# Layer 0 attention of a two-layer trunk: where projection units, modulation products and the turns at a head's end stand in TensorE's order

## The reference, cut to what matters

```python
mod = (silu(c) @ ada_w[l] + ada_b[l])[:, None, :]
h = rmsnorm(x, norm_g[l, 0]) * (1 + sc1) + sh1
proj = h @ w_in                       # even_mixer
# A: two score maps per head
s = where(causal, s - slope * dist, -inf); p = softmax(s)
w = p[:, :, 0] - lam * p[:, :, 1]
ya = rmsnorm(einsum(w, v), subln_g) * (1.0 - lam_init)
# B: dilated attention over three branches, heads in pairs
y = concatenate([ya, yb], axis=-1) @ w_out
```

## Time and profile before

| | us |
|---|---|
| median of 3 runs | 2991.62 (2991.14 to 2992.17) |
| profiled execution | 2992.33 |
| its span, first to last instruction | 2990.6 |
| mean granted clock of TensorE | 0.947 |
| layer 0's attention in the trace | about 106 to 663 |

### The profile page before, as it was taken

How to read it: one execution, slowest core, us unless ns; L and a number is a source line. 1 busy time by engine, 2 the same in 40 slices (tenths; PEclk the granted TensorE clock), 3 DMA queues, 4 the chain that set the end, 5 groups by cost and what they waited for, 6 DMA issues and landing times.

```text
span 2990.6 us, 35461 instructions
## 1 busy us (share of the span) xinstructions
PE 2687.0 (90%) x12576; PEld 2193.1 (73%) x12576; DVE 1261.9 (42%) x1451; ACT 1071.0 (36%) x1610; POOL 967.4 (32%) x402
## 2 busy tenths in 40 slices
PE   4999999989899999999999997666889999999995
PEld 2777778767678887788877786554667888788884
DVE  5566644333720155201567413766473005430145
ACT  2444443343433333333332223544343333322222
POOL 0111110004344444344434443211334444344442
PEclk7999999999899999999999998888999999999998
DMA  6233332043223332232346543111222333233232
GB/s 235 64 99 105 107 92 78 29 167 101 71 84 98 97 93 91 84 98 92 98 134 225 185 160 106 43 56 42 71 71 87 96 98 98 84 98 97 92 99 91
DMA packets 91097, 300.38 MB, mean 100 GB/s; under 512 B 9793, under 2 KB 10113, under 8 KB 91009
## 3 DMA queue, kind: packets, MB, share of 16 engines
q1 hardware_dynamic: 91008, 299.20, 31.4%
HBM read 275.05 MB, written 24.12 MB: 100 GB/s over the span
## 4 chain that ended last, share of the span: by engine, by line
issue 57%; PE 27%; POOL 11%; DVE 2%; DVEq 1%; ACT 1%; POOLq 1%; ACTq 0%
POOL w_lo L462 10%; PE ps L503 6%; PE ps L504 6%; PE ps L507 6%; PE ps L774 3%; PE ps L780 3%; PE ps L777 3%; POOL ybuf L473 1%; POOL arena L473 1%; DVEq L1222 0%; POOLq L476 0%; DVEq L1494 0%; DVE h_lo L1194 0%; ACT w_hi L828 0%; DVE ybuf L1186 0%
## 5 line engine op out<-in xcount | busy, mean ns | idle before, releaser
L462 POOL TENSOR_TENSOR w_lo<-w_raw,w_hi 128x1024 fp32r<-128x1024 f32 x370 | 909.4, 2461 | 1797.6 <-ACT w_hi L828 1293.5
L503 PE MATMUL ps<-h_hi,w_hi 128*128 128x512 f32 x2448 | 991.0, 405 | 85.8 <-ACT w_hi L828 54.7
L504 PE MATMUL ps<-h_lo,w_hi 128*128 128x512 f32 x2448 | 977.5, 399 | 0.0
L503 PEld LDWEIGHTS ps<-h_hi,w_hi 128*128 128x128 f32 x2448 | 474.6, 194 | 216.8 <-issue 78.3
L507 PE MATMUL ps<-h_hi,w_lo 128*128 128x512 f32 x2448 | 606.9, 390 | 0.0
L828 ACT ACTIVATE w_hi<-w_raw 128x1024 fp32r<-128x1024 f32 x346 | 363.9, 1057 | 632.0 <-PE ps L507 320.8
L504 PEld LDWEIGHTS ps<-h_lo,w_hi 128*128 128x128 f32 x2448 | 475.7, 194 | 97.0 <-issue 0.5
L507 PEld LDWEIGHTS ps<-h_hi,w_lo 128*128 128x128 f32 x2448 | 461.5, 189 | 96.4
L1598 DVE TENSOR_TENSOR arena<-arena,ps 128x512 f32 (+1 forms) x88 | 60.5, 688 | 782.6 <-PE ps L507 782.6
L1613 DVE TENSOR_TENSOR a_lo<-arena,a_hi 128x512 fp32r<-128x512 f32 x88 | 211.6, 2404 | 212.8 <-ACT a_hi L1149 212.5
L774 PE MATMUL ps<-a_hi,w_hi 128*128 128x512 f32 x704 | 174.3, 390 | 6.6 <-ACT a_hi L1149 6.6
(11 more groups left out here) (174 smaller groups left out, 2267.8 us busy)
## 6 DMA issues: line engine op xcount, KB each, us to landing
w_raw<-weights SPq DMA_DIRECT2D x370, 512.0 KB, 3.5
arena<-ada_w SPq DMA_DIRECT2D x80, 512.0 KB, 3.6
proj<-arena SPq DMA_DIRECT2D x24, 512.0 KB, 3.4
x<-xT SPq DMA_DIRECT2D x4, 2048.0 KB, 11.1
arena<-ada_w SPq DMA_DIRECT2D x4, 2048.0 KB, 20.2
arena<-proj SPq DMA_DIRECT2D x8, 1024.0 KB, 4.8
arena<-proj SPq DMA_DIRECT2D x8, 512.0 KB, 4.1
y_hi_d<-a_hi SPq DMA_DIRECT2D x7, 512.0 KB, 2.6
```

What stands on the lines that cost most here:

```text
L462: pool.tensor_tensor(w_lo[:, s, :], w_raw[:, s, :], w_hi[:, s, :].bitcast(f32), ALU.subtract).then_inc(lo_done, 1)
L503: pe.matmul(bank(b), w, high[:, k, :], start=k == 0, stop=False)
L504: pe.matmul(bank(b), w, low[:, k, :], start=False, stop=False)
```

## The change

The order of the work in layer 0's attention is changed, nothing else.

- Only the first four units of the next head stand whole, in row blocks 0 to 3. The fifth is cut into its three terms (`chunk_part`): w_hi with h_hi at the end of row block 5, w_hi with h_lo at the end of row block 6, w_lo with h_hi in row block 7 behind its turn. The sixth stands behind weigh(7).
- scores(0) of the next head stand ahead of weigh(7), scores(1) behind the sixth unit; then come the output turn and, behind it, the v turn. ScalarE's `exps(b+1, 0)` and VectorE's `biased(b+1, 0)` move into the head's end accordingly, and `copy_v` stands behind the output's two parts. ScalarE copies turn(7) before `output(6)`.
- `ada_turn` is gone. Its eight products (`ada_column`, L550 of the changed kernel) are dealt out over the first unit of heads 1 to 6, one after each pair of matmuls, in columns 448 to 455 of bank 6. `columns` is read one row block later, and the eight `ada_step` run as 0, 0, 2, 2, 1, 1, 1, 1 in row blocks 0 to 7.
- ScalarE makes w_hi of the unit weight 3b+7 at the head's end instead of row block 7.

```diff
+            def chunk_part(c, part):
+
+                u, half = chunk_of(c)
+                if part == 0:
+                    chunk_bank_free(c)
+                    pe.wait_ge(hi_done, u + 1)
+                if part == 2:
+                    pe.wait_ge(lo_done, u + 3)
+                w, h = ((w_hi, hh), (w_hi, hl), (w_lo, hh))[part]
+                for k in range(KB):
+                    mm = pe.matmul(bank(7), w[:, u % 2, k * P:(k + 1) * P], h[half][:, k, :],
+                                   start=part == k == 0, stop=part == 2 and k == KB - 1)
+                if part == 2:
+                    mm.then_inc(ch_done, 1)
+
+            def ada_column(n, m):
+
+                if m == 0:
+                    pe.wait_ge(acc_done, n + 1)
+                    pe.wait_ge(mod_done, n)
+                    pe.wait_ge(o_done, 8 * n + 1)
+                mm = pe.matmul(bank(6)[:, ADA_COL + m:ADA_COL + m + 1], acc_one[:, m * P:(m + 1) * P], ones[:, 0:1], start=True, stop=True)
+                if m == KB - 1:
+                    mm.then_inc(ada_mm, 1)
...
-                scores(1, b, slot)
+                ahead = 6 * (b + 1)
                 for n in range(8):
                     if kind == 1:
                         turn_weights(n)
+                        if n == 7 and not last:
+                            chunk_part(ahead + 4, 2)
                         if n:
                             weigh(n - 1)
                     if n < 6:
                         scores(n + 2, b, slot)
                     if kind == 0:
                         turn_weights(n)
+                        if n == 7:
+                            chunk_part(ahead + 4, 2)
                         if n:
                             weigh(n - 1)
                     elif n > 3:
                         turn_weights(n, 1)
-                    if n < 6 and not last:
-                        chunk(6 * (b + 1) + n)
-                        if (b, n) == (6, 5):
-                            pe.drain().then_inc(unit_used, 24)
+                    if not last:
+                        if n < 4:
+                            chunk(ahead + n, b if n == 0 and 0 < b < 7 else None)
+                        elif n in (5, 6):
+                            chunk_part(ahead + 4, n - 5)
+                if not last:
+                    scores(0, b + 1, 1 - slot)
                 weigh(7)
                 if not last:
-                    turn_v(b + 1, before(LANE[kind]))
-                    scores(0, b + 1, 1 - slot)
+                    for part in range(3):
+                        chunk_part(ahead + 5, part)
+                    if b == 6:
+                        pe.drain().then_inc(unit_used, 24)
+                    scores(1, b + 1, 1 - slot)
                 turn_out()
+                if not last:
+                    turn_v(b + 1, before(LANE[kind] + 1))
...
-                    exps(1)
+                    exps(b, 1)
                     for n in range(1, 8):
                         copies(n - 1)
                         if n > 1:
                             output(n - 2)
                         if n < 7:
-                            exps(n + 1)
-                        if n < 7 and not last:
+                            exps(b, n + 1)
+                        if n < 5 and not last:
                             evict(6 * (b + 1) + n - 1)
                         if n == 3 and not last:
                             hi_u(3 * b + 5)
-                        if n in (5, 7) and b < 6:
-                            hi_u(3 * b + 6 + n // 6)
...
+                        if n == 5 and b < 6:
+                            hi_u(3 * b + 6)
                     if kind == 0:
                         load_sqrt()
+                    copies(7)
                     output(6)
-                    copies(7)
+                    if not last:
+                        evict(6 * (b + 1) + 4)
                     output(7)
...
                     if not last:
-                        copy_v(b + 1, before(LANE[kind]))
+                        exps(b + 1, 0)
+                        evict(6 * (b + 1) + 5)
+                    if b < 6:
+                        hi_u(3 * b + 7)
...
                         if n < 7:
-                            biased(n + 1)
-                        if n == 0 and 0 < b < 7:
+                            biased(kind, b, n + 1)
+                        if n == 1 and 0 < b < 7:
                             columns(b, b + 1, 1)
...
                         if b < 6:
-                            ada_step(8 * b + n)
+                            for e in ((), (), (0, 1), (2, 3), (4,), (5,), (6,), (7,))[n]:
+                                ada_step(8 * b + e)
...
                     if not last:
                         biases((b + 1) // 4)
+                        biased((b + 1) // 4, b + 1, 0)
```

More of the change, by code:

```diff
@@ L490, in _, with unit @@
             pe.sem_inc(pv_done, 1)
[L492 removed]
+            def unit(use, s, b, job=None, high=h_hi, low=h_lo, y_new=False, done=unit_used, ada=None):
                 pe.wait_ge(hi_done, use + 1)
@@ L504, in unit @@
                     pe.matmul(bank(b), w, low[:, k, :], start=False, stop=False)
+                    if ada is not None:
+                        ada_column(ada, k)
                 pe.wait_ge(lo_done, use + 3)
@@ L508, in unit, with chunk_bank_free @@
                 mm.then_inc(done, 1)
-            def chunk(c):
-                u, half = chunk_of(c)
+            def chunk_bank_free(c):
                 if c > 1:
@@ L518, in chunk @@
                         pe.wait_ge(v_out, v_count(before))
-                unit(u, u % 2, chunk_bank(c), half if c in (0, 2) else None, hh[half], hl[half], done=ch_done)
+            def chunk(c, ada=None):
+                u, half = chunk_of(c)
+                chunk_bank_free(c)
+                unit(u, u % 2, chunk_bank(c), half if c in (0, 2) else None, hh[half], hl[half], done=ch_done, ada=ada)
+            def chunk_part(c, part):
+                u, half = chunk_of(c)
+                if part == 0:
+                    chunk_bank_free(c)
+                    pe.wait_ge(hi_done, u + 1)
[15 more added lines that the diff above has]
+                    mm.then_inc(ada_mm, 1)
             def two_pairs(use, tiles, i, job, down_before=None):
@@ L649, in turn_out @@
                     for lane in range(2):
-                        pe.wait_ge((ta_free, td_free)[lane], before(LANE[kind] + (not last)))
+                        pe.wait_ge((ta_free, td_free)[lane], before(LANE[kind]))
                         for n in range(4):
@@ L941, in copy_v, with exps @@
                     a.activation(v_tok[:, 0:4, :], bank(4).rearrange("p (m q) -> p m q", q=P), ACT.Copy).then_inc(ta_free, 1)
+                def exps(b, n):
+                    for c in range(2):
+                        a.wait_ge(nm_done, 8 * b + n + 1)
+                        K = P * (n + 1)
+                        a.activation(pr[n % 2][:, c, 0:K], pr[n % 2][:, c, 0:K], ACT.Exp, bias=nmx[:, 2 * n + c:2 * n + c + 1],
+                                     accum_out=rs[:, 2 * n + c:2 * n + c + 1]).then_inc(exp_done, 1)
                 def block_(kind, b, slot, last):
@@ L1012, in block_ @@
                     for half in range(2):
-                        a.wait_ge((ta_done, td_done)[half], before(LANE[kind] + (not last)))
+                        a.wait_ge((ta_done, td_done)[half], before(LANE[kind]))
                         dst = hh[half][:, b, :] if last else y_st_hi[:, half * HALF:(half + 1) * HALF]
@@ L1016, in block_ @@
                                      **({} if kind else {"scale": sub_g})).then_inc(y_hi, 1)
+                    if not last:
+                        copy_v(b + 1, before(LANE[kind] + 1))
                 copy_v(0, 1)
+                exps(0, 0)
                 for b in range(HEADS):
@@ L1267, in columns @@
                 w = 8 * groups
-                v.tensor_tensor(mod[:, 8 * first:8 * first + w], bank(6, w), ada_b[:, 8 * first:8 * first + w], ALU.add)
+                col = 6 * 512 + (ADA_COL if 0 < n < 7 else 0)
+                v.tensor_tensor(mod[:, 8 * first:8 * first + w], ps[:, col:col + w], ada_b[:, 8 * first:8 * first + w], ALU.add)
                 v.drain()
@@ L1349, in copy_v, with biased @@
                     v.tensor_copy(v_tok[:, 4:8, :], bank(5).rearrange("p (m q) -> p m q", q=P)).then_inc(td_free, 1)
+                def biased(kind, b, n):
+                    for c in range(2):
+                        K = P * (n + 1)
+                        col = 2 * n + c
+                        v.wait_ge(s_done[c], 8 * b + n + 1)
+                        if n > 1:
+                            v.wait_ge(ta_done, events(b, lane_count(kind, n - 1, 0)))
+                            v.wait_ge(td_done, events(b, lane_count(kind, n - 1, 1)))
+                        v.sem_inc(waited, 1)
```

(9 more changed lines are left out.)

34 lines of the change are left out of this document (5 added, 29 removed).

## The result

The changed kernel takes **3037.01 us** (3032.42 to 3039.77, four runs) beside 2991.89 (2991.14 to 2992.84) for the kernel before on the same chip: a ratio of 1.0149 [1.0132, 1.0167]. It is slower, as forecast, but 20 us more than forecast and 3 us beyond the range. The profiled execution took 3035.84 us.

A forecast was written before the change was run, and what follows sets the result against it. TensorE, busy 90% of the span, bounds the kernel. 4 x 0.4 + 3 x 0.3 + 17.5 + 5 = 25 us on the profiled 2992.33 (0.7 above the median 2991.62) gave 3016.6 us; range 2973 to 3034.

The forecast's parts named there:

- the price of a clock fall with the products in the unit: Next head's first unit after a clock fall at the head's end: 1.74 us more, plus 1.84 for products at full clock.
- The bound for the products, 3.41 us: Upper bound for the eight modulation products in the first unit, at half clock; 1.84 us was taken, lower bound nothing.
- the doubled sums: Two modulation sums in each of row blocks 2 and 3 delay VectorE's biased passes by 0.3 us, bounds 0 to 1.28.
- Scores(7) 2.5 forecast: A head: new TensorE wait of 2.5 us ahead of scores(7), for VectorE's biased passes of row block 6.
- Turn(6) 2.5: A head: new TensorE wait of 2.5 us ahead of the turn of row block 6, for VectorE's combined weights.
- V turn 1.85: End of an A head: new 1.85 us wait ahead of the v turn, behind ScalarE's eviction, w_hi and copy, and VectorE's subtraction.
- Scores(2) 2.1: End of an A head: 2.1 us wait ahead of scores(2), while VectorE copies v, drains and makes biased(1).
- In the first B head: B heads: waits ahead of turn(5), turn(6, second part), weigh(7), v turn and scores(2), +0.3 us per head at full clock.
- The rival with a full clock: Clock stays full throughout, so only 2.5 us are added: 2994 us; chance 0.15.
- The 3039 us rival: Clock also falls mid-head, twice in every A head and once in B: 47.5 us added, 3039 us; chance 0.15.
- The rule on weight loads: Weight loads pulled ahead of running matmuls would make part of the products' 1.84 us vanish, up to 11 us over six heads.
- The faster rival: Waits in row blocks 5 and 6 do not open: 2966 us at full clock, 2983 with falls at the ends; chance 0.22.

The follow-up runs named there:

- experiment 3: Changed kernel with the modulation products in one block between output turn and v turn, and single sums per row block: 2999.20 us, ratio 1.0022.
- experiment 6: Changed kernel with the modulation products dealt over the second unit instead of the first, read one row block later: 3019.25 us, ratio 1.0090.
- experiment 2: Kernel before with only the modulation products dealt over the first unit, sums and their reading as in the change: 3029.38 us, ratio 1.0134.
- experiment 4: Changed kernel with the modulation sums dealt 0, 2, 1, 1, 1, 1, 1, 1 over row blocks 0 to 7: 3023.90 us, ratio 1.0104.
- Experiments 8 to 10: Changed kernel, products in a block, scores(2) ahead of v turn; biased(1) behind normalisation 2972.31 us; row blocks 4 to 6 covered 2969.59; also w_hi moved 2966.08.
- experiment 10: Changed kernel with units in row blocks 4 to 6, scores(1), products, scores(2) ahead of output turn, w_hi of 3b+7 behind v copy: 2966.08 us.
- experiment 12: Changed kernel with the second pair of modulation sums in row block 4 instead of 3: 3029.92 us, ratio 1.0128.

## Why the prediction was right, and where it was wrong

- **Direction, right; size, 20 us short.** 25 us were forecast on the profiled execution, 43.5 came (3035.84 - 2992.33), and the median lies outside the range of 2973 to 3034.
- **The step that failed: the price of a clock fall with the products in the unit.** The prediction took 1.74 us for a first unit from a B head, whose unit had no products in it, and added 1.84 for the products at full clock, so 9.24 us, where 12.6 were measured in the mean. Both prices are right apart: a plain first unit takes 6.5 to 7.8 us in experiment 3, a product between pairs at full clock costs (0.69 - 0.47) = 0.22 us, 1.8 for eight (in experiment 6, 1.9 to 2.3). Together they are not: the unit stays at half clock to the end of its products, 13.0 to 13.8 us in five heads of six. 75.6 measured less 55.4 forecast is 20.2 us, and the miss on the profiled execution is 43.5 - 25 = 18.5; that the errors of the other terms come to so little together is luck. Experiments 2, 3 and 6 show it from three sides. The bound for the products, 3.41 us, was no bound: it priced them at half clock, but not the wide products beside them.
- **The second term mis-sized: the doubled sums.** Taken as a delay of 0.3 us with bounds 0 to 1.28; the pair alone is 2.05 us longer than two sums. The waits from scores(6) to turn(6) sum to 5.1 us in the second head (0.25 + 0.48 + 3.31 + 1.05), where 5.2 stood in the forecast, and to 6.9, 6.3 and 5.6 in the other A heads. In experiment 4 they are 3.4 in the second and 4.5 to 4.8 in the others. The sum of the rows was nearly met since the forecast had placed scores(7) and turn(6) a little late. What was missed is what these waits do to the clock: in the change it also falls in the middle of the A heads, over 20 us in all (at most 10 us of time, 5 forecast).
- **Near, term by term.** Scores(7) 2.5 forecast, 3.31 measured and 1.98 with the sums undone. Turn(6) 2.5, measured 2.28, 1.05, 2.30 and 1.59. None ahead of turn(7) and the output turn. Weigh(7) 0.4, measured 0.35. V turn 1.85, measured 1.52. Scores(2) 2.1, measured 2.02 to 2.38 at the three ends between A heads. The sum that leads to the start of the first unit, 247.6 + 0.9 + 0.4 + 0.14, is 249.0 and not 248.9: 0.6 us over four heads. In the first B head 0.50, 1.53, 0.72, 0.50 and 1.36 where 0.5, 1.4, 0.9, 0.8 and 1.8 stood; only scores(2), 0.76 against 1.9, was off (with 0.30 and 0.34 us more ahead of two first turns before it).
- **The rival with a full clock is out.** The clock fell at all heads' ends, with no wait longer than 3.31 us in the attention. By the rule of the Trainium skill that was named for it (TensorE: Matmul & The Clock Gate, HAM oscillation — how this bites in real kernels) it should not have; the trace disagrees.
- **The 3039 us rival met the number, not the mechanism.** It had 2.5 us for each of 11 falls in the middle of heads, 27.5 us. There were falls in the A heads alone, worth 10 us at most; the rest came from the dealt products. A number that fits does not bear out its story.
- **The rule on weight loads** of the Trainium skill (TensorE: Matmul & The Clock Gate, Step-by-step: what each phase is for) would have let the products vanish in part. In experiment 6, at clock 1.00, the unit takes 8.0 us against 5.7 without them in A heads, and 7.4 against 5.6 in B heads: nothing of the 1.84 vanished.
- **The faster rival is out** for the changed kernel (scores(7) waits in every A head). Experiments 8 to 10 show that a gain of the size it named is there, 20 to 26 us, by another way: the waits go from 45 to 30 us and the half clock from 68 to 27 in experiment 10, and neither is gone. That its 2966.08 us meets the rival's 2966 is chance, since the rival had a full clock throughout.

Left open: why the dealt unit of one head (8.44 us, head 3) got its clock back within a few pairs, and five did not. Other versions with dealt products show the same two outcomes at other heads (8.51 and 9.18 in experiment 2, 8.63 in experiment 4, 8.33 in experiment 12; a unit of 7.46 in experiment 12 was at full clock throughout). No run tells what decides it. The runs of experiment 2 lie from 3024.80 to 3035.82 us, so the number of held units may differ between executions, which is not shown. Nor was it tried which property of the products holds the clock: their one column, their own weights, or their place after every pair.

## What to carry to other kernels

Short, narrow products that are dealt between wide ones cost little at full clock, and, here in most heads, a great deal where the engine comes out of a wait at half clock; put them where the engine would wait anyway, or behind a plain stretch. Price a piece of work at the clock it will find, together with its neighbours, and not as a sum of parts each from its own row. When work is taken out of a place, ask what it covered: the best version here puts units back into the row blocks that had lost them, and work of TensorE and VectorE into the waits at the heads' ends.

## What the runs showed of the hardware that was not expected

- **One-column products between 512-wide ones held the half clock.** At half clock a pair of matmuls with a product takes 1.28 us, at full clock 0.69. In five heads of six the dealt units stayed at a granted clock of 0.50 for all eight, TensorE's lower level of 1.2 GHz, with the engine busy 13.90 of 13.90 us. A plain unit in the same place was at 0.74 in the mean over 7.4 us (experiment 3). Behind a plain unit that had brought the clock back, the same dealt products ran at 1.00 in all six heads (experiment 6).
- **A sum on VectorE of two operands in SBUF and a subtraction on GpSimd slow each other.** The second sum of the pair took 3.25 us instead of 1.28, GpSimd's w_lo 3.14 instead of 2.36. With the pair a row block away, all 42 sums took 1264 to 1286 ns (experiment 12), but w_lo still took 3.15, as in the kernel before: there too a single sum is issued 0.39 us ahead of it, and only w_lo pays. The Trainium skill (SBUF — State Buffer, Who interferes with whom) says that a VectorE instruction with two inputs in SBUF and a GpSimd instruction that reads SBUF share a port pair as an exclusive lock, and that the order of issue decides who blocks. The trace agrees: w_lo, from 213.64, began beside the first sum (213.25 to 214.52) and took 0.78 us more than its 2.36; it ended at 216.78, and the second sum, which began at 214.62, only at 217.87, 1.09 us behind it.
- **A version's parts do not add.** The doubled sums cost 5.5 us in one setting and 13 in another. They add 7.1 and 7.3 us of waits there, but 3.4 and 13.6 us of half clock.
